# RWKV projections with the key and decay preparation in one stage, head normalization by token halves, and another order of loads in sample attention

## What is computed

```
xr, xw, xk, xv, xa, xg = (xn + xx * mu[i] for i in range(6))
r = xr @ w_r
k = xk @ w_k
v = xv @ w_v
w_log = -jax.nn.softplus(-(w0 + jnp.tanh(xw @ w1) @ w2).astype(F32)) - 0.5
a = jax.nn.sigmoid((a0 + (xa @ a1) @ a2).astype(F32))
g = jax.nn.sigmoid(xg @ g1) @ g2
...
kk = k * k_k.astype(F32).reshape(RW_HEADS, RW_HEAD)
kk = kk / jnp.maximum(jnp.sqrt(jnp.sum(kk * kk, axis=-1, keepdims=True)), 1e-12)
k = k * (1.0 + (a - 1.0) * k_a.astype(F32).reshape(RW_HEADS, RW_HEAD))
...
mean = jnp.mean(o, axis=-1, keepdims=True)
var = jnp.mean(jnp.square(o - mean), axis=-1, keepdims=True)
o = ((o - mean) * lax.rsqrt(var + RW_GN_EPS)).reshape(B, T, D) * gn_w.astype(F32) + gn_b.astype(F32)
bonus = jnp.sum(r * k * r_k.astype(F32), axis=-1, keepdims=True) * v
o = (o + bonus.reshape(B, T, D)).astype(xn.dtype)
return (o * g) @ w_o, s_T
```

## Time and profile before

| | |
|---|---|
| Runs | 2798.35 us median of 3 (2790.52 to 2799.75) |
| Profiled execution | 2799.37 us, span 2797.7 us |
| PE busy | 2165.5 us (77% of the span) |
| DVE busy | 957.4 us (34%) |
| ACT, POOL busy | 499.0 us, 506.2 us (18% each) |
| Mean granted TensorE clock | 0.876 of full speed |

### The profile page before, as it was taken

One profiled execution on the slowest core, in us unless ns is written; L12 is line 12 of the kernel. 1 busy time (PEld: TensorE's weight loads), 2 busy tenths in 40 slices (PEclk: granted clock), 3 DMA queues, 4 the chain that ended last, 5 costly groups with the idle time before them and its releaser, 6 DMA issues. The chain is left out here.

```text
span 2797.7 us, 44940 instructions
## 1 busy us (share of the span) xinstructions
PE 2165.5 (77%) x17469; PEld 1433.2 (51%) x17469; DVE 957.4 (34%) x1713; ACT 499.0 (18%) x1123; POOL 506.2 (18%) x562
## 2 busy tenths in 40 slices
PE   3999521799848489996866968878889996499994
PEld 2787410799736433333755745544445565433333
DVE  4101597444272212222122156643335412212123
ACT  0001220122210011110000025543334300111110
POOL 0332132222010133332000033310000000223331
PEclk8999755899959589997986969999999998599997
DMA  1885001300011669991332120034545652489962
GB/s 41 261 257 168 4 0 67 128 4 4 7 30 30 216 253 380 377 366 70 83 92 62 39 81 2 2 121 143 159 142 171 215 157 62 171 347 375 379 272 96
DMA packets 240020, 407.96 MB, mean 146 GB/s; under 512 B 56418, under 2 KB 193923, under 8 KB 213820
## 3 DMA queue, kind: packets, MB, share of 16 engines
q1 hardware_dynamic: 193900, 350.05, 35.1%
q0 software_dynamic: 38656, 50.83, 5.7%
q10 hardware_dynamic: 7264, 4.36, 0.5%
HBM read 499.44 MB, written 79.44 MB: 207 GB/s over the span
## 5 line engine op out<-in xcount | busy, mean ns | idle before, releaser
L394 PE MATMUL banks<-slots,work 128*128 128x260 f32 x1920 | 431.6, 388 | 11.6 <-DMA work<-in_rw_wv 2.6
L394 PEld LDWEIGHTS banks<-slots,work 128*128 128x128 f32 x1920 | 370.5, 193 | 71.7 <-issue 13.4
L1515 PE MATMUL banks<-slots,work 128*64 128x512 f32 x1536 | 342.6, 599 | 0.5 <-DMA slots<-in_moe_wup,overflow_weight_rows 0.2
L2454 PE MATMUL banks<-slots 128*128 128x508 f32 x512 | 250.9, 605 | 8.7 <-ACT work L2554 7.4
L1515 PEld LDWEIGHTS banks<-slots,work 128*64 128x64 f32 x1536 | 106.4, 138 | 203.0 <-issue 201.7
L1541 PE MATMUL banks<-slots,work 128*64 128x512 f32 x768 | 175.3, 598 | 3.6 <-DVE work L1593 3.6
L2525 DVE COPY slots<-banks 64x256 f32<-64x256 f32 x256 | 109.3, 427 | 193.9 <-PE banks L2359 189.6
L1227 POOL DMA_INDIRECT expert_lists<-work x20 | 19.5, 977 | 712.9 <-DVEq L238 707.4
L905 PE MATMUL banks<-slots 64*64 64x64 f32 x3840 | 138.3, 223 | 5.8 <-DMA small<-in_consts 4.6
L905 PEld LDWEIGHTS banks<-slots 64*64 64x64 f32 x3840 | 133.3, 139 | 7.0 <-DMA small<-in_consts 4.7
L1579 DVE TENSOR_TENSOR work<-work,banks 128x256 f32<-128x256 f32 x48 | 29.2, 607 | 306.8 <-ACT work L1561 306.8
(11 more groups left out here) (380 smaller groups left out, 2973.1 us busy)
## 6 DMA issues: line engine op xcount, KB each, us to landing
slots<-in_moe_wgate SPq DMA_DIRECT2D x64, 1024.0 KB, 14.8
slots<-in_moe_wup SPq DMA_DIRECT2D x64, 1024.0 KB, 17.0
slots<-in_moe_wdown SPq DMA_DIRECT2D x64, 1024.0 KB, 12.8
sample_cache_rows<-in_cache_kv POOLq DMA_DIRECT2D x128, 256.0 KB
slots<-in_cache_kv SPq DMA_DIRECT2D x256, 128.0 KB, 2.3
slots<-sample_cache_rows SPq DMA_DIRECT2D x32, 512.0 KB, 5.8
slots<-sample_cache_rows SPq DMA_DIRECT2D x64, 256.0 KB, 5.9
slots<-expert_result_rows SPq DMA_DIRECT2D x8, 1024.0 KB, 7.7
```

The source lines that it names most:

```text
L394: last = nc.tensor.matmul(c.pair[u][0:out_rows, s, :], ring[u][:, k, :], x[:, k, HALF * s:HALF * s + HALF], start=(k == 0), stop=(k == kt ...
L1515: last = mm(c.bank[v][SEAT * j:SEAT * j + SEAT, :], xt[v][:, k, SEAT * j:SEAT * j + SEAT], weights.gate_up_of[2 * s + j][:, k], start=(k = ...
L2454: last = mm(HIDDEN[:, 0:KVH * NCMP_S], s.w1[:, u // NB, j, :], s.xt[u % 2][:, :, j % 8, first:first + NCMP_S], start=(j == 0), stop=(j == 15))
```

## The change

1. **Low rank comes first and holds the differences.** "shift" is gone. DVE takes the difference tile by tile and mixes w and a behind it; g, k, r and v follow. PE puts the first products of w and a into the two halves of the same output, alternating, and their second products come from the two halves of the contraction rows. SP loads the first two weight tiles of the projections here.
2. **One stage "rwkv_projections"** replaces three projections, prepare and scale. Its 24 tiles run in the order k, r, v from a ring of two. Behind each tile PE does one small pair of matmuls: sums of squares of k into 16 rows, one per head (`headsel`), the spread of their inverse to 128 rows (`headback`), and the bonus sums. There is one clamp, root and reciprocal of 16 x 520 instead of eight of 128 x 520. POOL's products go to DVE, and POOL issues all 128 page copies here. The bonus is given bias and gate at once.
3. **Arrays move**: r, v and o, the chunk buffers, sample vectors (two stores in place of one) lie elsewhere.
4. **Head normalization** works by halves of 260 tokens: centring is a matmul with a matrix of identity less 1/64, squares on ACT, sums in 16 rows, weight and gate in one DVE operation on the centred PSUM tile, one inversion per half, spread by PE, one product and one sum per tile on DVE. POOL does nothing.
5. **Sample attention**: the pages of a unit are issued ahead of the keys.

```diff
+    sel = np.zeros((P, 30)); sel[0:HD, 14] = 1; sel[HD:P, 15] = 1
+    put("headsel", sel)
+    back = np.zeros((NH, KT, P))
+    for h in range(NH):
+        back[h, h // 2, HD * (h % 2):HD * (h % 2) + HD] = 1
+    put("headback", back.reshape(NH, -1))
...
+    def load_tile(sp, t):
+        m = t % KT
+        sp.dma_start(ring[t % 2], weight[t // KT][:, :, P * m:P * m + P]).then_inc(tile_in[t % 2], 16)
...
+            for t in range(2):
+                load_tile(sp, t)
...
-            for x, (n, m) in enumerate(order):
-                rows = pairs[n][2]
-                if x >= 4:
...
-                    for k in range(KT):
-                        for s in range(2):
-                            last = nc.tensor.matmul(pair[0:rows, s, :], first[n][:, k, :],
-                                                    mixed(3 + n)[:, k, HALF * s:HALF * s + HALF],
-                                                    start=(k == 0), stop=(k == KT - 1))
...
+            mm = nc.tensor.matmul
+            pe.wait_ge(loaded_w, 32)
+            pe.wait_ge(loaded_a, 32)
+            for k in range(KT):
+                pe.wait_ge(wa_mixed, k + 1)
+                for s in range(2):
+                    mm(c.pair[0][0:HD, s, :], first_w[:, k, :], mixed["w"][:, k, span(s)], start=(k == 0), stop=(k == KT - 1))
+                    last = mm(c.pair[0][HD:P, s, :], first_a[:, k, :], mixed["a"][:, k, span(s)], start=(k == 0),
+                              stop=(k == KT - 1))
+            last.then_inc(wa_first, 1)
...
+            nc.vector.tensor_scalar(xx[:, :, 0:1], xn[:, :, 0:1], -1.0, None, ALU.mult)
+            tt(xx[:, :, TP:NT], xx[:, :, TP:NT], xn[:, :, TP:NT], ALU.subtract)
+            for k in range(KT):
+                tt(xx[:, k, 1:TP], xn[:, k, 0:TP - 1], xn[:, k, 1:TP], ALU.subtract)
+                dve.drain()
+                mix("w", k)
+                mix("a", k).then_inc(wa_mixed, 1)
+            for k in range(KT):
+                last = mix("g", k)
+            last.then_inc(g_mixed, 1)
+            for k in range(KT):
+                mix("k", k)
+            dve.wait_ge(wa_first, 1)
+            for name in ("r", "v"):
+                for k in range(KT):
+                    mix(name, k)
...
+    with c.stage("rwkv_projections") as st:
...
+            table = lambda name, rows=P: io["consts"][0:rows, CCOL[name][0]:CCOL[name][1]]
+            sp.dma_start(keep, table("keep")).then_inc(constants_in, 16)
+            sp.dma_start(to_head, table("headsel")).then_inc(constants_in, 16)
+            for n in range(2):
+                sp.dma_start(of_head[n], table("headback", NH)[:, 512 * n:512 * n + 512]).then_inc(constants_in, 16)
+            for t in range(2, NTILES):
+                sp.wait_ge(done, t - 1)
+                load_tile(sp, t)
+        @block.gpsimd
+        def _(pool):
+            c.copy_pages(pool, range(NB * NPG))
...
+            def sum_squares(k):
+                pe.wait_ge(squared, k + 1)
+                for s in range(2):
+                    last = mm(c.pair[2][0:NH, s, :], to_head[:, 14 - 2 * k:30 - 2 * k], square[k % 2][:, span(s)],
+                              start=(k == 0), stop=(k == KT - 1))
+                last.then_inc(summed, 1)
...
+            pe.wait_ge(constants_in, 64)
+            for t in range(NTILES):
+                tile(t)
+                if 1 <= t < KT + 1:
+                    sum_squares(t - 1)
+                if KT + 1 <= t < 2 * KT + 1:
+                    spread_inverse(t - KT - 1)
+                if t >= 2 * KT + 1:
+                    sum_bonus(t - 2 * KT - 1)
+            sum_bonus(KT - 1)
...
-                nc.vector.tensor_scalar(w[:, j, :], w[:, j, :], NLOG, None, ALU.mult)
-                dve.drain()
-                nc.vector.tensor_tensor_scan(tmp[:, j, 0:TP], keep, w[:, j, 0:TP], 0.0, ALU.mult, ALU.add)
...
-                dve.wait_ge(roots, j + 1)
-                nc.vector.reciprocal(norm[j % 2], norm[j % 2]).then_inc(inverted, 1)
...
+                ts(w[:, k, :], w[:, k, :], NLOG, None, ALU.mult)
+                ts(factor[k % 2], a[:, k, :], -1.0, c.vec("ka", k), ALU.add, ALU.mult)
+                dve.drain()
+                nc.vector.tensor_tensor_scan(cum[:, k, prompt], keep, w[:, k, prompt], 0.0, ALU.mult, ALU.add)
+                dve.drain()
+                nc.vector.tensor_copy(ends[:, k, :], cum[:, k, CH - 1:TP:CH])
+                tt(w[:, k, prompt], cum[:, k, prompt], w[:, k, prompt], ALU.subtract).then_inc(decays, 1)
+                dve.wait_ge(moved, k + 1)
+                ts(kk[:, k, :], k_[:, k, :], c.vec("kk", k), None, ALU.mult)
+                stt(k_[:, k, :], factor[k % 2], 1.0, k_[:, k, :], ALU.add, ALU.mult)
+                if k >= 2:
+                    dve.wait_ge(summed, k - 1)
+                dve.drain()
+                tt(square[k % 2], kk[:, k, :], kk[:, k, :], ALU.mult).then_inc(squared, 1)
+            dve.wait_ge(summed, KT)
+            ts(halves(inverse), c.pair[2][0:NH], 1e-24, None, ALU.max).then_inc(clamped, 1)
+            dve.wait_ge(rooted, 1)
+            nc.vector.reciprocal(inverse, inverse).then_inc(inverted, 1)
...
```

The second and third rounds over k in this stage scale kk, r, w, a and k by the spread inverse and the exponentials, and form the bonus, as before but on DVE alone. Of the head normalization and of the rest:

```diff
-                    nc.vector.scalar_tensor_tensor(halves(centred[:, k, :]), c.pair[k % 2], -1.0 / HD, halves(o[:, k, :]),
-                                                   ALU.mult, ALU.add).then_inc(centred_ready, 1)
...
-                    nc.vector.scalar_tensor_tensor(o[:, j, :], normed[:, j, :], c.vec("lnw", j), bonus[:, j, :],
-                                                   ALU.mult, ALU.add)
-                    dve.drain()
-                    nc.vector.scalar_tensor_tensor(o[:, j, :], o[:, j, :], c.vec("lnb", j), g[:, j, :],
-                                                   ALU.add, ALU.mult)
...
+            def gate(x):
+                s, k = steps[x]
+                dve.wait_ge(squared, x + 1)
+                nc.vector.scalar_tensor_tensor(scaled[:, k, span(s)], CENTRED[x % 4][:, 0:HALF], c.vec("lnw", k),
+                                               g[:, k, span(s)], ALU.mult, ALU.mult).then_inc(gated, 1)
+            def invert(s):
+                dve.wait_ge(summed, KT * (s + 1))
+                nc.vector.tensor_scalar(inverse[s], SUMS[s][0:NH, 0:HALF], 1.0 / HD, GN_EPS, ALU.mult,
+                                        ALU.add).then_inc(variance, 1)
+                dve.wait_ge(rooted, s + 1)
+                nc.vector.reciprocal(inverse[s], inverse[s]).then_inc(inverted, 1)
...
+            def multiply(x):
+                s, k = steps[x]
+                dve.wait_ge(spread, x + 1)
+                nc.vector.tensor_tensor(scaled[:, k, span(s)], scaled[:, k, span(s)], SPREAD[x % 2][:, 0:HALF],
+                                        ALU.mult).then_inc(multiplied, 1)
+                dve.drain()
+                nc.vector.tensor_tensor(o[:, k, span(s)], scaled[:, k, span(s)], bonus[:, k, span(s)], ALU.add)
...
+            nc.vector.scalar_tensor_tensor(centre, c.headones, -1.0 / HD, c.ident, ALU.mult, ALU.add)
+            dve.drain().then_inc(centring, 1)
+            for x in range(KT + 2):
+                gate(x)
+            invert(0)
+            for x in range(KT + 2, 2 * KT):
+                multiply(x - KT - 2)
+                gate(x)
+            invert(1)
+            for x in range(KT - 2, 2 * KT):
+                multiply(x)
...
             for u in range(UNITS):
+                load_pages(2 * u + 4)
+                load_pages(2 * u + 5)
                 if u + 2 < GROUPS:
                     load_keys(u + 2)
-                load_pages(2 * u + 4)
-                load_pages(2 * u + 5)
...
     rwkv_inputs(c)
-    rwkv_prepare(c)
     sample_state(c)
```

More of the change, by code:

```diff
@@ L500, in mixed @@
[L500 to L516, removed]
@@ L517, in rwkv_inputs @@
-    first = [c.work[:, 1024 * n:1024 * n + KT * pairs[n][2]].rearrange("p (k n) -> p k n", k=KT) for n in range(3)]
-    second = [c.work[0:pairs[n][2], 3072 + D * n:3072 + D * n + D] for n in range(3)]
-    hidden = [c.work[0:pairs[n][2], 6144 + NT * n:6144 + NT * n + NT] for n in range(3)]
-    order = [(0, None), (1, None)] + [(0, m) for m in range(KT)] + [(2, None)]
-    order += [(n, m) for n in (1, 2) for m in range(KT)]
-    halves = lambda a: a.rearrange("p (s t) -> p s t", s=2)
-    with c.stage("low_rank") as st:
-        loaded = [st.sem(f"weights_loaded{n}") for n in range(3)]
-        mix_ready, full, free = st.sem("input_mixed"), st.sem("product_in_psum"), st.sem("product_taken")
+    mixed = {"w": c.slot(3), "a": c.slot(4), "g": c.slot(5), "k": c.slot(6), "r": c.slot(3), "v": c.slot(4)}
@@ L580, in rwkv_prepare, with mix @@
-def rwkv_prepare(c):
-    nc, io = c.nc, c.io
-    r, k_, v, w, a = (c.slot(n) for n in range(4, 9))
-    kk, tmp, bonus = c.slot(1), c.slot(2), c.slot(3)
-    keep = c.work[:, 0:TP]
-    norm = [c.work[:, TP + NT * n:TP + NT * (n + 1)] for n in range(2)]
+            tt, mixing = nc.vector.tensor_tensor, nc.vector.scalar_tensor_tensor
```

(16 more changed lines are left out.)

426 lines of the change are left out of this document (233 added, 193 removed).

## The result

The changed kernel takes **2630.99 us** (median of 4 runs, 2625.30 to 2637.39) against 2799.05 (median of 4 runs of the kernel before). The ratio is 0.9412, 95% interval 0.9391 to 0.9432, so it is faster by 168 us. The forecast was 2625 with a range of 2604 to 2660. The profiled execution took 2632.92, its span is 2631.3, which is 166.4 less than before.

The account below looks back on a forecast made before the run. Bound: about 311 us on two jobs using PE and DVE one after the other. Terms -17.7 (low rank), -111.5 (projections), +0.5 (sample vectors), -26.6 (normalization), -19 (attention) sum to -174.3: 2799.4 becomes 2625, range 2604 to 2660.

Parts of the forecast that it names:

- The fused projection stage is PE's, with DVE under it: Projections, prepare and scale as one stage: PE's chain sets its 199.7 us, DVE's work hides; gain 111.5 from 311.2.
- one wait for weights (0.4) took the place of 2: Projection stage: waits for weight loads with two buffers instead of four, between 0 and 7 us, taken as 2.
- I count 0: Projection stage: PE's 32 tile-shape changes there and back cost nothing; by the skill's rule 5 in all, forecast 2630.
- Copies on POOL: Projection stage: POOL issues all 128 pages, one every 1.13 us, 145 in all, well inside 199.7.
- the rival fell: Rival: DVE operations stop POOL from issuing, so copies end the projection stage at 222, total 2647; chance 0.04.
- Low rank, 44.4 forecast: Differences and low rank in one stage, 62.1 us before, to take 44.4 with the barrier; gain 17.7.
- the table load that I had them hide behind: Low rank: a table load of 1.3 us, after tanh and copy of 1.2, before the first sigmoid at 19.9.
- Six rounds, ... 1.35 each: 8.1: Head normalization: six rounds of three matmuls, DVE much the same, 8.1 us of the stage's 38.7; stage gain 26.6.
- The rival with the slow normalization (58): Rival: the head normalization waits often at a low clock, 58 us instead of 38.7, total 2644; chance 0.12.
- Sample attention, 19 forecast with bounds 8 and 23: Pages issued ahead of keys remove PE's page waits, 28.7 us in 17 cases, except 6.5 and some 3; gain 19.
- The paired rival: Rival: low rank's paired products do not overlap, 10.5 us worse, total 2636; chance 0.04.
- the rival of SP's order: Rival: sample attention's new SP order buys nothing, PE waiting for the second eight pages instead, total 2644; chance 0.09.

## Why the prediction was right, and where it was not

- **The fused projection stage is PE's, with DVE under it:** right. Clock 0.99, DVE 88.5 of 203.6, and 16 us more of DVE changed nothing. The constants took the 3.9 forecast, one wait for weights (0.4) took the place of 2, and the first tiles cost 1.9 for the low clock instead of 2.6.
- **"I count 0" for PE's changes of shape:** wrong. The term measures 5.5 for 32 changes. I had read the ends of records, which overlap what follows. Starts show it in the earlier trace rows already: ten records of 508 columns at 0.428 (508 / 260 of 0.219) are 4.28, and the next row starts after 4.35; 16 records of 512 columns, four side by side, are 1.72, and the next row starts after 1.86. So my reading that they join without a gap was wrong. The Trainium skill (TensorEngine Tiling (Array Packing), Key Properties) says that a change of mode drains the engine; my estimate from it and the rows was 5, and these runs agree with it.
- **Copies on POOL:** right, and the rival fell. They follow each other by 1.13 and the last is issued at 259.3, three quarters into the stage.
- **Low rank, 44.4 forecast, 48.3 measured:** the mechanism was right (in PE's timeline the products of w and a start in pairs within 0.04 of each other), the sizes were off. Mixing took 1.3 longer; PE, which waits for each mix, ran at a clock of 0.81 in this stage, so the last first products took 2.0 instead of 0.9, and the first second products, at the same clock, came 0.9 later than the table load that I had them hide behind; ACT's 16 took 10.6 instead of 10.0. The 1.1 and the 0.9, 2.0 together, come from the clock and vary: from SP's first load to its first of the next stage, the stage took 48.4 to 48.5 in five of the eight profiled kernels that have it unedited, the changed one among them, at 0.81 or 0.82, and 46.5 in three, at 0.89. One of the three, the kernel with both shapes full in the normalization:

```profile
56.34:102.83 46.49, 32.71 (x192) 22.85 (x192) 38.03 (x58) 18.98 (x29) 0.00 (x0) 0.89 0.28 69
```

- **Head normalization:** here the forecast failed, in the step "Six rounds, ... 1.35 each: 8.1". They took 18.5 (657.4 to 675.9), since the clock fell behind the first inversion and three changes of shape stood in each round. At 1.81, the round at the full clock, six would be 10.9: some 2.8 of the 10.4 too much are the shapes and the rest is the clock. Until the tenth gate the stage took 14.6 as forecast (14.7), and behind the second inversion 9.0 (8.7 forecast). With full shapes it took 38.6, what I had forecast for the narrow ones. The rival with the slow normalization (58) was half right: I gave it all or nothing. Its 58 also does not come out of the rows that the forecast used: 17.5 for the ten steps and 15.8 for the six rounds at the low clock, with the rest as forecast, give 52.5. Two of my own signs speak against the forecast here: I had named a clock near 0.6 as a sign of being wrong, and it was 0.64, and the stage lies outside the 35 to 45 that I named as right.
- **Sample attention, 19 forecast with bounds 8 and 23, 27.8 measured:** the order did what was forecast, but the size was too small in two steps. The later units' waits went as well, so 20.9 went and not 19; and the 7 of PE's own time behind the waits (half of it the lower clock behind two of them, half the slower first product behind each) were not in the sum at all. The bound of 23 held only waits, and so wasn't one.
- **The paired rival, the rival of SP's order and the slow rival** did not come about: the projections kept 0.99.

## What to carry to other kernels

Work of two engines that stands in two stages is worth nearly the whole of the shorter one when it is put under the longer, and the room left is measured by adding idle work to the hidden engine. Small products between large ones were cheaper here at the full 128*128 shape than at 16 rows or columns, even if seven eighths of them are zeros: the shape keeps the rate and, where spreads of 16 rows left the clock low behind a pause, full ones got it back. The price is a larger table, which comes later. A wait of PE costs more than its own length: in sample attention 0.2 more for the first product behind each, and some 1.7 more where the clock fell, which was behind two of 16.

## What was not expected

The rows of busy times of the changed kernel's normalization, from where the clock rose to the end of the pause, and of the rounds from where it fell:

```profile
645.10:656.60 11.50, 9.27 (x32) 3.04 (x31) 5.50 (x9) 4.68 (x10) 0.00 (x0) 1.00 0.00 0
658.70:676.00 17.30, 17.30 (x33) 5.56 (x33) 6.39 (x17) 1.55 (x4) 0.00 (x0) 0.50 0.00 1
```

In the rounds PE is busy 17.30 of 17.30 and yet granted 0.50, while spreads of 16 rows stood among its products; with full shapes alone the clock was back after 3.4. In the first row sums of 16 columns stood between the centring products, and there the clock had risen and stayed at 1.00, so not every narrow product keeps it down. What exactly decides was not tried further: a pause of 2.7 with full shapes brought the clock down three times and left it up once.
